# Whole-array products of ones on TensorE: behind norms, in front of output projections and inside the first attention

## The reference, cut to what matters

```python
def hybrid_layer(x, ...):                       # first model, depth 1
    proj = rmsnorm(x, norm1_w) @ w_in
    y_a = dilated_attention(...)                # 6 heads of 64, three dilated causal branches
    y_b = gla(...)                              # gated linear attention, 4 heads, chunks of 16
    y_c = moba_attention(...)                   # 6 heads of 64, with 512 tokens: causal
    x = x + concatenate([y_a, y_b, y_c]) @ w_out
    return x + square(relu(rmsnorm(x, norm2_w) @ w_ff1)) @ w_ff2

for l in range(2):                              # second model
    ux, uc = (rmsnorm_2(x) * (1 + sc_a) + sh_a) @ w_in[l], (...ctx...) @ w_in[l]
    fx, ax, rx = fourier_mix(...), attention_group(...), hgrn_group(...)
    x = x + g_a * (concatenate([fx, ax, rx]) @ w_out[l])
    x = x + g_f * swiglu(rmsnorm_2(x) * (1 + sc_f) + sh_f, w_gate[l], w_up[l], w_down[l])
    ...                                         # the same for ctx in layer 0
return rmsnorm_2(x, final_norm)
```

## Time and profile before

| | |
|---|---|
| three runs | 2568.95, 2574.23 and 2745.06 us; median 2574.23 |
| profiled execution, its own time | 2582.34 us |
| its span, first to last instruction | 2580.6 us |
| mean granted clock of TensorE | 0.939 |
| PE busy | 2409.3 us, 93% |
| PEld, DVE, POOL, ACT busy | 71%, 40%, 31%, 30% |

### The profile page before, as it was taken

How to read it: one execution, slowest core, us unless ns; L and a number is a source line. 1 busy time by engine, 2 the same in 40 slices (tenths; PEclk the granted TensorE clock), 3 DMA queues, 4 the chain that set the end, 5 groups by cost and what they waited for, 6 DMA issues and landing times.

```text
span 2580.6 us, 35232 instructions
## 1 busy us (share of the span) xinstructions
PE 2409.3 (93%) x15254; PEld 1839.2 (71%) x15254; DVE 1035.7 (40%) x1475; ACT 777.5 (30%) x953; POOL 802.8 (31%) x279
## 2 busy tenths in 40 slices
PE   7987899999999999889899999999799989899998
PEld 5763367777887883458788888888487446688886
DVE  7654446255255426622523323312452743311113
ACT  4322233123234314423311121112433533322222
POOL 3322243333442214302222222222222413343432
PEclk9985699999999998889999999999899879999999
DMA  6530034443222101012023322311211003222221
GB/s 217 187 123 18 17 138 156 163 163 116 98 73 92 42 1 48 2 51 74 33 98 115 115 98 83 146 54 37 92 41 48 2 2 114 82 98 98 98 90 57
DMA packets 36411, 218.11 MB, mean 85 GB/s; under 512 B 4152, under 2 KB 7016, under 8 KB 13088
## 3 DMA queue, kind: packets, MB, share of 16 engines
q1 hardware_dynamic: 32968, 209.44, 22.5%
q10 hardware_dynamic: 3288, 6.41, 0.7%
HBM read 213.70 MB, written 2.14 MB: 84 GB/s over the span
## 4 chain that ended last, share of the span: by engine, by line
PE 77%; DVE 6%; ACT 3%; issue 1%; POOL 1%; DMA 0%; DVEq 0%; ACTq 0%; POOLq 0%
PE PS L739 61%; PE PS L1228 2%; PE PS L1255 2%; PE PS L754 2%; DVE s_states L1635 1%; DVE a_lo L661 1%; DVE tmp L668 1%; PE PS L1940 1%; PE PS L1832 1%; PE PS L1272 1%; PE PS L2053 1%; PE PS L1240 1%; PE PS L849 1%; ACT w_hi L917 1%; DVE x L681 1%
## 5 line engine op out<-in xcount | busy, mean ns | idle before, releaser
L2189 POOL TENSOR_TENSOR w_lo<-raw,w_hi 128x2048 fp32r<-128x2048 f32 (+3 forms) x163 | 666.0, 4091 | 1464.0 <-ACT w_hi L917 1464.0
L739 PE MATMUL PS<-a_hi,w_hi 128*128 128x512 f32 (+1 forms) x2104 | 695.0, 372 | 45.3 <-DVE a_lo L661 25.3
L739 PE MATMUL PS<-a_lo,w_hi 128*128 128x512 f32 (+1 forms) x2104 | 685.3, 367 | 0.0
L739 PE MATMUL PS<-a_hi,w_lo 128*128 128x512 f32 (+1 forms) x2104 | 683.3, 366 | 0.0
L739 PEld LDWEIGHTS PS<-a_hi,w_hi 128*128 128x128 f32 x2104 | 367.6, 191 | 130.4 <-issue 54.5
L739 PEld LDWEIGHTS PS<-a_hi,w_lo 128*128 128x128 f32 x2104 | 365.1, 191 | 66.7
L739 PEld LDWEIGHTS PS<-a_lo,w_hi 128*128 128x128 f32 x2104 | 364.4, 191 | 63.3 <-issue 1.7
L917 ACT ACTIVATE w_hi<-raw 128x2048 fp32r<-128x2048 f32 (+1 forms) x145 | 270.3, 1864 | 324.3 <-PE PS L739 114.6
L739 PE MATMUL PS<-hid_hi,w_hi 128*128 128x512 f32 (+1 forms) x784 | 259.3, 367 | 1.6 <-issue 1.6
L739 PE MATMUL PS<-hid_hi,w_lo 128*128 128x512 f32 (+1 forms) x784 | 258.9, 366 | 0.0
L739 PE MATMUL PS<-hid_lo,w_hi 128*128 128x512 f32 (+1 forms) x784 | 258.4, 366 | 0.0
(11 more groups left out here) (228 smaller groups left out, 2339.7 us busy)
## 6 DMA issues: line engine op xcount, KB each, us to landing
raw<-in_w_ada SPq DMA_DIRECT2D x48, 1024.0 KB, 6.8
raw<-in_w_ff SPq DMA_DIRECT2D x32, 1024.0 KB, 4.9
raw<-in_w_in SPq DMA_DIRECT2D x22, 1024.0 KB, 4.9
raw<-in_w_gate SPq DMA_DIRECT2D x22, 1024.0 KB, 4.9
raw<-in_w_up SPq DMA_DIRECT2D x22, 1024.0 KB, 5.0
raw<-in_w_down SPq DMA_DIRECT2D x16, 1024.0 KB, 4.8
raw<-in_w_out SPq DMA_DIRECT2D x12, 1024.0 KB, 5.0
raw<-in_w_down SPq DMA_DIRECT2D x8, 768.0 KB, 4.2
```

Of the source, the lines that this page charges most:

```text
L739: mm = p.matmul(ps[:, dst], wv[:, k, idx * P:(idx + 1) * P], av[:, k, dst], start=first, stop=last)
L2189: pool.tensor_tensor(low[:, ks, :], whole[:, ks, :], high[:, ks, :].bitcast(F32), ALU.subtract).then_inc(tell.sem, 1)
```

## The change

A helper `keep_busy(p, ps, n)` issues n products of `ones_r` (128x128) with `ones_r` read four times over (128x512) into a PSUM bank that the next real product overwrites. Nobody waits for them and they tell no semaphore. They are put at five kinds of place: behind the slot waits of the first panel of `out1`, `out2_0`, `out2_1` (11 each); behind those of `in1` (7), `ff1_0` (13), `ff2_0_0`, `in2_1`, `ff2_1_0` (15 each); two in front of each of the units 8 to 47 of the first attention; 20 in front of its unit 0; and 4 in each of the last three steps of its last group, behind a wait for the bank.

```diff
+        FILL_BEHIND = {"in1": 7, "out1": 11, "ff1_0": 13, "ff2_0_0": 15, "in2_1": 15, "out2_0": 11, "out2_1": 11, "ff2_1_0": 15}
+
+        def keep_busy(p, ps, n):
+            for _ in range(n):
+                p.matmul(ps[:, 0:SEQ], ones_r[:], ones_r[:].unsqueeze(1).to_broadcast([P, SEQ // P, P]), start=True, stop=True)
...
                 if rising is not None and name.startswith("out"):
                     for n in job_of[i]:
                         slot_free(n)
+                    keep_busy(p, slot(job_of[i][0]), FILL_BEHIND[name])
                     for k in range(kt):
                         p.wait_ge(rising.sem, rising.at(k + 1))
...
                     last_part = sides[-1]
                     for n in job_of[i]:
                         slot_free(n)
+                    keep_busy(p, slot(job_of[i][0]), FILL_BEHIND.get(name, 0))
...
                 ps = scores_ps(plan, u)
+                if u >= plan["end_unit"][0]:
+                    keep_busy(p, ps, 2)
...
+            if causal:
+                keep_busy(p, scores_ps(plan, 0), 20)
             for u in plan["units_at"][0]:
                 scores(u)
...
                     for u in plan["units_at"][2 * s + 1]:
                         scores(u)
+                    if causal and steps[s][0] == len(groups) - 1 and not steps[s][2]:
+                        bank_free(("sum", len(groups) - 1))
+                        keep_busy(p, sums_ps(plan, 0), 4)
```

## The result

The three runs of the changed kernel took 2588.65 to 2591.45 us, median 2591.27; before, 2574.23. The ratio is 1.0062 with a 95% interval of 1.0034 to 1.0089; it is taken without the run of 2745.06 us, as all ratios here leave out the few runs in a slower state of the chip. So the time is within 2%, which had most of the chance, but its sign is the other one, and it lies just above the range of 2508 to 2590.

The account below looks back on a forecast made before the run. It took TensorE at half clock in the first attention as the bound. Norms 0, output projections +2 and attention -26 gave -24 us: 2582 - 24 = 2558, 8 less for a median, 2550 us; range 2508 to 2590.

Parts of the forecast that it names:

- What bounds it: Whole kernel: the last chain is mostly TensorE's, and its clock is lost in the first attention, 194 to 323 us.
- The attention's price: First attention: 64 products at 0.22 us add 14 us in four groups; fifth group +0.5, sixth +1.
- I hide none: First attention's first four groups: none of the 64 products' 14 us is taken as hidden in TensorE's waits.
- The attention's gain: First attention's first four groups: a raised clock saves 45 us of TensorE's busy time, nine tenths taken, 41 us.
- the tenth that was set aside: First four groups: 41 us taken of 45, because the clock must rise first and will still fall at some group's end.
- (a): Rival: the clock doesn't rise in the first attention, so the products only cost: +38, 2612 us; chance 0.12.
- (b): Rival: the first attention's clock rises half of the time, 22 us regained, 20 paid: about 2575 us; chance 0.14.
- (c): Rival: first four groups fall to the fifth's period, 45 us gained, nothing paid: 2531 us, down to 2515; chance 0.24.
- A rule against the change: First attention: by the skill's keep-busy rule, a stage 80 to 95% busy is already fast; added products are price alone.
- Behind the norms: Five sites behind norms: products fit in waits, the panel still waits for DVE; 0 us, bounds -2 and +2.
- In front of the output projections: 11 products each behind the w_lo wait: out1 +2.4, out2_0 -1.4, out2_1 +1.0, together +2 us.
- The start and the last group: First attention: 20 products before unit 0 hide in a 5.38 us wait, 0; 12 in the sixth group, +1 us.

Follow-up runs that it names:

- pairs_4rows: pairs_only with each added product reading 4 of the array's 128 rows: 2623.33 us against 2572.96 for the kernel before, ratio 1.0183.
- pairs_only: The kernel before with only the two products in front of each of units 8 to 47 of the first attention: 2590.91 us, ratio 1.0069.
- norms_only: The kernel before with only the products behind the five norms: 2568.67 us against 2574.29, ratio 0.9985.
- start_last_only: The kernel before with only the 20 products at the first attention's start and the 12 in its last group: 2578.71 us, ratio 1.0018.
- fours_only: pairs_only with four products in front of each score in place of two: 2597.17 us against 2572.96 for the kernel before, ratio 1.0082.

## Why the prediction was wrong, step by step

**What bounds it: right.** The first attention was the place where the clock was lost, and of the added products it was the fed rows, not busy time, that raised it (pairs_4rows).

**The attention's price: wrong, and one of the two steps that turned the sign.** The prediction took 64 x 0.22 = 14 us for the first four groups and +1.5 net for the others. Measured: the 68 products of those groups (the first period holds ten scores, not eight) cost about 32 us of busy time, 0.47 each, and all 92 about 39. The 0.22 came from the earlier trace rows, 90 products in an unbroken stream. Inside the attention a pair stands alone between other products. At full clock the pair and the score behind it start 0.66 us apart, behind a wait (194.35 and 195.01) and without one (196.39 and 197.05), in a few places 0.55; at half clock 0.98 to 1.15. That is some 0.33 and 0.49 to 0.58 for one product. The half-clock distance of 0.43 was in the text, but for the attention only in a rival. The sentence "I hide none" was right, and the idle time that the products could not use is the 1.18 us in front of them.

The Trainium skill (TensorE: Matmul & The Clock Gate, section "Wait — 56ns, not 53.3ns?") gives 215.7 ns from start to start for back-to-back products of 512 columns at full clock. Rows 4 agree with 0.22; the attention's 0.33 is no stream of back-to-back products and lies outside what that sentence covers.

**The attention's gain: wrong in size, and the other of the two.** Nine tenths of 45 us were to come back in the first four groups; about 24 did. As a ceiling the 45 is right (46 by the same count), and the halving itself holds (8.0 against 7.9 above). What failed is the tenth that was set aside because "the clock has to rise first and will still fall at some group's end". It fell five times: at about 212.5, 226.1, 263.6, 277.2 and 301.2 us, two of them at a group's end, and each time TensorE stood in a wait of 0.9 to 2.2 us then or shortly before, for DVE's maximum or ACT's `acc` (three other waits, of 1.1 to 1.3 us, as the one that ended at 194.35, were followed by no fall). Twice it then stayed low, for 27 and for 20 us, through the stretches of the gated scan, in which no added product stands for 9 us at a time (from 231.3 to 240.0, and from 283.4 to 293.1). The wait in front of the second fall, the low stretch behind it, and 128 of the scan's products elsewhere:

```profile
223.15:225.35 2.20, 0.00 (x1) 0.00 (x0) 2.15 (x5) 1.43 (x4) 2.05 (x2) 1.00 0.00 0
226.10:253.30 27.20, 21.30 (x305) 11.09 (x305) 8.54 (x24) 4.39 (x9) 3.19 (x5) 0.50 0.07 20
256.09:257.49 1.40, 1.40 (x129) 1.27 (x128) 0.94 (x4) 0.00 (x0) 0.22 (x1) 1.00 0.05 12
```

That the waits cause the falls is not shown: in pairs_only one fall, at 286.2 us, came behind 4.8 us of the scan's products and no wait. Granted clocks of 0.85 to 1.00 were forecast for four groups and came in one. The four periods, 26.98 to 36.40 us, are all above 26, the mark at which the prediction called itself wrong.

**Together.** In the first four groups +9.6 us where -27 stood: 17 us of missing gain (24 for 41), 18 of price (32 for 14) and 2 of idle time. With only the gain right they would have come to about -7, with only the price right to about -8: it took both to turn the sign. The fifth group grew by 2.2 us where +0.5 was forecast, and the start and the sixth came out at -0.1 and -0.2 instead of 0 and +1; that makes the +11.5.

**The rivals.** (a) said that the clock doesn't rise, below about 0.65: it rose, though to no more than 0.73 over the four groups. (b) came nearest: it has 22 us regained, which is close to the 24, and 20 paid, as it used 0.32 for a product; with the 32 measured it is 12 us longer, some 2587, of the 2591 that came. (c) fell: no period came near the 16.08 us of the fifth group before.

**A rule against the change.** The stretch at 0.50 with 5.00 us busy is at 1.00 now with 4.92 busy, and the same number of products on 4 rows leaves the clock at 0.54. The Trainium skill (the same page, section "Why this matters for your kernels") asks for TensorE to be kept busy without gaps; in these runs busy records alone don't raise the clock. By that rule pairs_4rows, with 90% of the stretch busy, would have been fast in most of it. For the time, though, the rule's verdict that the products are a price alone was nearer than the forecast.

**Behind the norms: right.** TensorE's timeline behind `ff1_0`'s norm, against the earlier trace rows:

```profile
400.43 3.24 PE L706 MATMUL PS<-ones_r 128*128 128x512 f32 x13
404.20 0.50 PE L747 MATMUL PS<-a_hi,w_hi 128*128 128x512 f32 x1 [0.54 <-DVE a_lo L661]
...
408.26 0.50 PE L747 MATMUL PS<-a_hi,w_hi 128*128 128x512 f32 x1 [0.83 <-DVE a_lo L661]
...
411.64 0.50 PE L747 MATMUL PS<-a_hi,w_hi 128*128 128x512 f32 x1 [1.72 <-DVE a_lo L661]
```

The wait of 3.71 became 3.2 us of products and 0.54 of wait. Behind it the panel runs at full clock (1.00 from 404 to 412 us) and waits for DVE's `a_lo`, more and more, as forecast. The stretch from norm to norm went from 208.39 to 207.47 us, and norms_only is at 0.9985 with 1 in its interval.

**In front of the output projections: right, nearly term by term, with +2.4, -1.4 and +1.0 forecast.** `out1`, `out2_0` and `out2_1`, from the first `a_lo` to the next norm, and then the added products of `out1` with the `w_lo` in front of them, against the earlier trace rows:

```profile
342.87:397.72 54.85, 53.22 (x268) 41.09 (x268) 26.35 (x22) 16.89 (x19) 19.62 (x5) 0.94 0.42 154
1179.19:1247.68 68.49, 68.49 (x395) 59.73 (x394) 21.44 (x28) 21.32 (x26) 18.47 (x4) 1.00 0.24 84
2155.51:2204.57 49.06, 47.76 (x204) 39.38 (x205) 18.12 (x21) 16.89 (x19) 19.50 (x5) 0.97 0.28 93
```

```profile
339.57 4.52 POOL L2206 TENSOR_TENSOR w_lo<-raw,w_hi 128x2048 fp32r<-128x2048 f32 x1 [0.91 <-ACT w_hi L927]
344.44 2.90 PE L706 MATMUL PS<-ones_r 128*128 128x512 f32 x6 [4.56 <-POOL w_lo L2206]
```

Before, the three took 53.03, 70.54 and 46.98 us. So +1.8, -2.0 and +2.1, together +1.9 for the +2 forecast; `out2_0` has no dip left, at 1.00. At `out1` TensorE idles 4.56 us for `w_lo` and only then starts the products that were to fill a wait (the last row shows six of the eleven); its first real product starts at 349.15 us, 5.1 behind the end of `w_lo`, where it had been 0.7; 3 to 5 later was forecast.

**The start and the last group:** about 0 and +1 forecast; start_last_only has +0.7 us in the stretch and 1.0018 (1.0001 to 1.0034) overall.

## What to carry to other kernels

Price a filler product where it will stand: in front of the instruction it holds up it costs its start-to-start there (here 0.33 us at full, 0.49 to 0.58 at half clock), not the 0.22 of a stream, and it is paid each time unless TensorE would have waited anyway. A raised clock gave back about half of the busy time that it reached and nothing of the waits; ask how much of the stage it will reach, and compare that with the number of products times this price, dose by dose, before anything else. In these runs filler came free only ahead of a wait, as behind the norms, and once per wait; behind the wait it was added time.

## What the runs showed of the hardware that was not expected

Full-array products raise the clock, 4-row products over the same columns don't (0.80 against 0.54), although TensorE is busy for 90% of the stretch with them and for 82% without. One whole-array product per score left it at 0.60, two brought 0.80, four 0.87: the response isn't in proportion. In the change the clock stayed at 0.50 through two stretches of small products of the scan although TensorE was busy for 7.68 of 8.00 us in one of them. But such products also ran at 1.00: 128 of them at 256.09 us in the change, 126 at 233.89 us in fours_only. They don't halve with the clock: 128 of one kind (`s_att`) took 2.69 us at half clock and 1.82 at full (fours_only, from 287.38 us).
